# A split moved nine points later in each head, and a token difference moved ahead of three low parts in merge

## What is computed

```
h = rms_norm(x, g_norm) * (1 + scale) + shift
xa, va, oa, za, ia, fa, qa, ka, vat, zb, ga, gb = split(h @ w_in)
xc  = silu(conv(xa));  q_m, k_m = xc @ w_q, xc @ w_k;  h_m = mlstm_chunkwise(q_m, k_m, va, ia, fa)
y_m = ((rms_norm(sigmoid(oa) * h_m) + skip * xc) * silu(za)) @ w_out_mlstm
o_a = softmax over groups of dilated_window_attention(rotary(qa), rotary(ka), vat)
y_a = (o_a * silu(zb)) @ w_out_attn
x   = rms_norm(x + gate * ((sigmoid(ga) * y_m + sigmoid(gb) * y_a) @ w_out), g_final)
```

## Time and profile before

| | before |
|---|---|
| median of 3 runs | 1365.64 us (1365.32 to 1367.71) |
| the profiled execution's own time | 1365.64 us |
| span of the profiled execution | 1363.8 us |
| mean granted PE clock | 0.997 |
| PE busy | 1337.2 us, 98% |
| DVE, ACT, POOL busy | 913.7, 594.6, 481.9 us |
| DMA | 171.22 MB, mean 126 GB/s |

### The profile page before, as it was taken

The page is one execution under the profiler, slowest core; times in us unless marked ns, Lnnn a source line. Parts: engine busy times, 40 slices in busy tenths (PEclk is TensorE's granted clock), DMA queues, the critical chain, the costliest instruction groups (busy, mean ns, idle before and its releaser), DMA issues. The chain is left out here.

```text
span 1363.8 us, 17501 instructions
## 1 busy us (share of the span) xinstructions
PE 1337.2 (98%) x6405; PEld 1120.5 (82%) x6405; DVE 913.7 (67%) x1511; ACT 594.6 (44%) x1039; POOL 481.9 (35%) x308
## 2 busy tenths in 40 slices
PE   8999999999999999999999999999999998999998
PEld 6888888888888888888888888888888886888786
DVE  7988766573744445535368856866876689669676
ACT  7663353344444344333545455354545543233122
POOL 0097555454554555542101200210120024542541
PEclk9999999999999999999999999999999999999999
DMA  9522323322234334327232741553272162246332
GB/s 333 182 80 96 131 102 124 124 93 104 112 124 139 124 127 151 139 108 216 84 90 63 217 93 32 167 144 94 63 209 70 33 217 77 93 136 231 112 93 93
DMA packets 63759, 171.22 MB, mean 126 GB/s; under 512 B 21809, under 2 KB 21937, under 8 KB 62390
## 3 DMA queue, kind: packets, MB, share of 16 engines
q1 hardware_dynamic: 60794, 162.44, 36.1%
q10 hardware_dynamic: 2880, 7.65, 1.9%
HBM read 127.38 MB, written 41.65 MB: 124 GB/s over the span
## 5 line engine op out<-in xcount | busy, mean ns | idle before, releaser
L1275 POOL TENSOR_TENSOR wlo<-wraw,whi 128x1024 fp32r<-128x1024 f32 x28 | 74.5, 2661 | 430.3 <-ACT whi L1495 406.1
L739 POOL TENSOR_TENSOR wlo<-w_sum,whi 128x512 fp32r<-128x512 f32 x112 | 164.8, 1473 | 137.2 <-ACT whi L864 137.2
L616 PE MATMUL banks<-t_hi,wlo 128*128 128x512 f32 x448 | 174.3, 389 | 0.0
L614 PE MATMUL banks<-t_hi,whi 128*128 128x512 f32 x448 | 174.3, 389 | 0.0
L615 PE MATMUL banks<-t_lo,whi 128*128 128x512 f32 x448 | 174.3, 389 | 0.0
L1010 DVE TENSOR_TENSOR c_sum<-c_sum,banks 128x512 f32<-128x512 f32 x196 | 134.4, 686 | 46.0 <-PE banks L616 32.0
L614 PE MATMUL banks<-h_hi,whi 128*128 128x512 f32 x416 | 162.1, 390 | 0.7 <-POOL wlo L1275 0.7
L616 PE MATMUL banks<-h_hi,wlo 128*128 128x512 f32 x416 | 161.9, 389 | 0.0
L615 PE MATMUL banks<-h_lo,whi 128*128 128x512 f32 x416 | 161.9, 389 | 0.0
L864 ACT ACTIVATE whi<-w_sum 128x512 fp32r<-128x512 f32 x112 | 70.5, 630 | 165.8 <-PE banks L616 100.7
L614 PE MATMUL banks<-whi,h_hi 128*128 128x512 f32 x256 | 99.9, 390 | 0.0
(11 more groups left out here) (410 smaller groups left out, 2975.2 us busy)
## 6 DMA issues: line engine op xcount, KB each, us to landing
wraw<-in_w_all SPq DMA_DIRECT2D x68, 512.0 KB, 4.4
raw<-in_w_all SPq DMA_DIRECT2D x28, 512.0 KB, 4.4
queries_keys<-fin SPq DMA_DIRECT2D x12, 1024.0 KB, 4.0
qa<-queries_keys SPq DMA_DIRECT2D x12, 768.0 KB, 11.9
s_wada<-in_w_ada_cols SPq DMA_DIRECT2D x16, 512.0 KB, 6.0
attn_values<-fin SPq DMA_DIRECT2D x6, 1024.0 KB, 4.0
tn<-attn_values SPq DMA_DIRECT2D x12, 512.0 KB, 9.1
merge_gates<-fin SPq DMA_DIRECT2D x5, 1024.0 KB, 3.9
```

Of the source, the lines that this page charges most:

```text
L614: t_.matmul(out, w_hi, x_hi, start=first, stop=False)
L616: return t_.matmul(out, w_lo, x_hi, start=False, stop=last)
L739: nc.gpsimd.tensor_tensor(wlo4[:, o % 4, :], source(r, j), whi4[:, o % 4, :].bitcast(F32), subtract).then_inc(s_split, 1)
L1275: nc.gpsimd.tensor_tensor(to, wraw[:, q % 2, :], hi.bitcast(F32), ALU.subtract).then_inc(w_split, 1)
```

## The change

In mix, next_high(n + 2) at the last part is now done for n > ZA only. The call for n = ZA (the next head's first chunk) stands at point TURN - 3 = 20 on ACT. In merge, DVE makes the third token difference (j = 7) right after that of j = 4, ahead of three low parts, and ACT makes its high part ahead of the loop over the products.

```diff
                         if part == PARTS_OF - 1:
                             keep(n, h)
-                            if h:
+                            if h and n > ZA:
                                 next_high(n + 2)
...
                         mixing(u)
+                        if u == TURN - 3:
+                            next_high(ZA + 2)
                         if u == TURN - 2:
                             z_sigmoid(ZA)
                             z_sigmoid(ZB)
...
         sum_high(4)
+        sum_high(7)
         for o in range(TOTAL, WITH_BRANCH):
...
-            if o == TOTAL:
-                sum_high(7)
...
         difference(4, low_left[0], bt_raw[6], 6)
+        difference(7, low_right[0], up_right)
         low(2, low_left[0])
         low(4, bt_raw[4])
         low(6, bt_raw[6])
-        difference(7, low_right[0], up_right)
         low(7, bt_raw[7])
```

## The result

The changed kernel takes 1379.62 us (median of 4 runs, 1378.66 to 1381.28), the kernel before 1365.68 us beside it (4 runs, 1365.32 to 1367.71): a ratio of 1.0101, 95% interval 1.0089 to 1.0113, so **+13.9 us** where +12.2 was forecast. The profiled execution took 1381.28 us, with a span of 1379.5 us and a mean granted clock of 0.994.

The account below looks back on a forecast made before the run. TensorE, busy 98% of the span, was taken as the bound, so only its waits could move the time. -4.8 + 13.2 + 9.3 - 5.5 = +12.2 on 1365.6 gave 1377.8 us, range 1369 to 1388.

Parts of the forecast that it names:

- Step 1: Point 11 of each head: the copy and split leave, L1729's collision and PE's wait for pT go; -4.8 us.
- Step 2: Point 20: POOL's moved split waits for the first L1752 of DVE, the second waits for POOL; split ends at 1093.7.
- The alternative of 1373.4 us: Point 20 with the port no limit: the bank is copied 1.1 us earlier in each head, sum 4.4 us lower.
- Step 3: SP's queue: the load waits for the moved split, szb lands late behind it, ACT copies the last bank 7.8 us later.
- Step 4: Ends of heads 0 to 2: PE waits 3.1 us for the bank, plus 1.3 from DVE; 4.4 per head, +13.2 us.
- The 1.3 us at the fold weights: Heads 0 to 2: DVE's delay around the fold weights' split makes L1700 late for PE, 1.3 us per head.
- Rival (a): Heads 0 to 2: POOL behind both L1752, PE pauses over 4 us and its clock halves; +12.2 more, 1390; chance 0.14.
- Step 5: Head 3 into merge, without cover: bank 7.4 us late, slow clock 2.6, a small wait gone 0.7; +9.3 us.
- a wait of 0.66 us: Merge at 1116.07: PE's wait behind ct goes, since PE is 10.0 us later and ct's chain some 7.8; -0.7 us.
- the six saves of statistics: SP's queue: these small saves move behind the split, said harmless because not needed before 1096.8.
- The slow clock was over-sized: Start of merge: after PE's longer pause, 15 matmuls take 6.0 us instead of 3.4; 2.6 us added.
- Step 6: Merge, product 7: the earlier third difference takes 2.9 us off PE's wait and 2.6 off the slow clock; -5.5 us.

Follow-up runs that it names:

- e4_point12: The changed kernel with the next head's copy and split at the start of point 12 instead of point 20, merge's new order kept: 1356.39 us.
- e1_merge_only: The kernel before with only merge's new order; the split stays at point 11: 1363.05 us, ratio 0.9979 to the kernel before.
- e5_szb_stats_first: The changed kernel with the gate rows and both saves of statistics issued ahead of the next head's load in SP's queue: 1368.46 us.
- e3: The changed kernel with only the gate rows (szb) issued ahead of the load in SP's queue: 1373.92 us.
- e7: e4_point12 with the gate rows issued later, behind the statistics saves and the head's last statistics: 1360.49 us.
- e2: The kernel before with only the split moved to point 20, merge as before: 1382.16 us, ratio 1.0120 to the kernel before.
- e8: e4_point12 unchanged, timed again beside e9 on one chip: 1356.95 us.
- e9: The changed kernel with the copy after the steps of point 17 (TURN - 6) instead of point 20: 1368.88 us.

## Why the prediction was right, step by step

The forecast was 1377.8 us, slower, in a range of 1369 to 1388; measured 1379.62.

**Step 1** held: no L1729 above 0.223 us, no wait for pT. Its size was 1.56 us per head (e4_point12 against e1_merge_only), 1.2 in the sum. That the 1.21 us of the row and PE's 1.28 us lie so near each other is chance: the delay was 1.21 and another 0.65 of ACT's copy, which the prediction doesn't name, less what DVE had to spare. At the end of the span the two kernels differ by 5.1 us and not by 6.2, because the slow clock at product 2 cost more in e4 (0.50) than in e1 (0.72).

**Step 2** came out as the row at point 11 had said: POOL waited for the first L1754, the second one for POOL. The pair grew by 2.17 us, nearly the length of the split. e5_szb_stats_first prices it alone, 2.2 us per head. This is also where the rule of the Trainium skill cited there ("SBUF — State Buffer", "Who interferes with whom") was put to use: the trace agrees, with 4.53 us for a pair of 2.36. The alternative of 1373.4 us, without the port, had only its effect on the gate rows; e5 shows that the port costs something even when the rows are in time, because PE's transposes wait for og.

**Step 3** held in its order and nearly in its size. ACT's copy of the last bank is 1108.37 - 1092.38 - 8.85 = 7.1 us later in head 3, 7.8 predicted; the sigmoid of szb began 0.5 us sooner than summed (1107.41 for 1099.1 + 8.85). e3 (moved forward) and e7 (moved back) show that it is szb and its place in the queue.

**Step 4**: 4.4 us per head predicted; against the 118.24 us of e4_point12 the three heads took 5.8, 4.7 and 4.6 us more, 15.0 together for the 13.2. The terms were otherwise: after head 1 PE is held first by og (2.05 us), then by the bank (1.46); 3.5 together for the 3.1 predicted. The 1.3 us at the fold weights did not appear: DVE's L1700 was in time, and instead the third chunk's split was late by 0.34. PE's starts there, laid beside those of e4, lose 2.2 us at the og wait, 1.8 at the bank, 0.6 at the third chunk and 0.1 after it. So each wait costs 0.1 to 0.3 us more than the idle time of its row, as in step 1; that time is counted from the end of the last matmul, 0.39 us after its start, where the next would have started after 0.23. Rival (a) put a slow clock behind a pause of over 4 us in each head. No such pause came, but behind the og wait of head 0 the clock was 0.73 all the same, and this is the head that took 1.1 us more than the other two.

**Step 5** was the one that failed in size. The start of merge came 15.7 us late, as summed (15.8), but by terms that made up for each other: -6.2 of step 1, +15.0 of step 4 and 6.9 for the start of merge, where -4.8, +13.2 and 7.4 stood. PE's one wait of about 7 us for the bank came as two, 2.06 for og and 4.42 for the bank. Then the sum let a wait of 0.66 us vanish, where one of 3.09 us stands. The sentence that failed is the one on the six saves of statistics, "not needed before 1096.8": ct needs them landed. They were issued at 1103.34 behind the split, ct came at 1115.07, 2.7 us after the load ahead of it and not 0.4, and took 11 us to land, 1.6 more than before. SP's own wait says for what:

```profile
SPq L1205 <- DMA softmax_stats<-st: 2.3, 1, 2.3
```

DVE waited 10.4 us for ct, and behind DVE stand ACT's exponential (L1572), ACT's next weight copy, POOL's split and PE. The slow clock was over-sized in turn: eight matmuls at 0.43 us in place of 0.23, 1.6 us and not 2.6. With the 8.85 us taken off, ct reached DVE 11.0 us later than before and PE was 8.5 us later, where the prediction had 7.8 and 10.0; 0.66 + 11.0 - 8.5 is the pause. The shift at the second pair is 19.8 us where steps 1 to 5 add to 17.7, and the slow clock behind this pause (0.72), which the sum doesn't have either, makes it 21.4.

**Step 6**: -5.5 predicted. In the change the shift falls from those 21.4 us to 15.7, -5.7; alone the merge part gave -2.9 by the medians and -4.1 in the profiled execution. ACT had the third high part done at 1164.83, 10.6 us before PE began product 7, and DVE came next, as said. What the sum leaves out for the merge part alone is the pause that moves forward to product 2. The change shows only 0.5 us of it, since PE was late already; in e1 and e4, with PE on time, it is 3.1 us.

So the loss was forecast from two rows: the collision at point 11, and the load issued 0.02 us after the split. The median is 1.8 us above the forecast. The profiled execution, the slowest of the four, is 3.5 us above it, and there the steps close: 2.1 up to the second pair's product, 1.6 for the slow clock behind it, -0.2 in step 6.

## What to carry to other kernels

A step moved in one engine's list takes with it everything that waits for it in a DMA queue: list what is issued behind it, and what is in order behind each receiver, down to stores whose landing a later load waits for. A freed collision is worth its price only at a place where all engines are free: against point 11 (e1_merge_only), one point later gained 6.7 us, six points later lost 5.8, nine points later 16.6. Cover that a next stage gives ends with the last repetition, so cost the last one apart.

## What the runs showed of the hardware

- DVE and POOL took turns by whole instructions where both worked on SBUF alone: 4.53 us for two products of 1.22, 3.40 for a split of 2.38. POOL got in between two back-to-back instructions of DVE.
- The small stores of statistics took up to 16.1 us to land where ACT's six loads were under way beside them (e3), and 6.7 at most in the kernel before. That these loads caused it was not tried alone.
- A pause of PE of 2 to 3 us cost clock in some executions and not in others, at one and the same place in the program. After the og wait of 2.05 to 2.11 us the 6 us behind it had 0.72 or 0.73 in head 0 of the changed kernel, in head 2 of e2, in heads 0, 1 and 3 of e3 and in head 2 of e5, and 1.00 in heads 1 and 2 of the changed kernel, in head 2 of e3 and in the other three of e5. Where it fell, the head took 1.6 us more in e3 and e5, and 1.1 in the changed kernel. After the 3.03 to 3.10 us at product 2 it was 0.50 in e4 and e8, 0.72 in e1 and e7 and 1.00 in e5. At merge it was 0.70 after 4.42 us, 0.77 after 2.85 and 0.72 after 2.54 (e9), and 1.00 after 2.93 (e7). After 1.3 to 1.6 us it never fell here. The rows don't tell what decides between them.

Two of these windows: e7 at the start of merge, then e4 at product 2.

```profile
1094.00:1100.00 6.00, 6.00 (x29) 4.95 (x28) 5.00 (x3) 1.68 (x2) 1.98 (x1) 1.00 0.99 373
```

```profile
1140.00:1146.00 6.00, 5.42 (x13) 4.31 (x14) 6.00 (x3) 2.40 (x3) 4.85 (x2) 0.50 0.01 3
```
